# A ninth slot, in two halves, for the ring of expert weights, and a new pairing of the mixing stage's weight buffers

## The reference, cut to what matters

```python
def hierarchical_moe(h, ...):          # T = 256 tokens, 32 experts, top 2 of one group of 8
    ...
    def expert_block(args):
        xb, e = args
        hid = jax.nn.silu(xb @ w_expert_gate[e]) * (xb @ w_expert_up[e])   # 1024 -> 512, twice
        return hid @ w_expert_down[e]                                      # 512 -> 1024
```

```python
    mixed = gates[..., :D] * y_att + gates[..., D:] * y_rwkv
    x = x + mixed @ w_out
```

## Time and profile before

| | us |
|---|---|
| median of 3 runs | 1432.18 |
| lowest and highest | 1431.21 and 1439.7 |
| the profiled execution | 1433.79 |
| its span on the core | 1432.0 |
| PE busy, DVE busy, ACT busy | 1213.7, 734.4, 480.7 |

### The profile page before, as it was taken

How to read it: one execution, slowest core, us unless ns; L and a number is a source line. 1 busy time by engine, 2 the same in 40 slices (tenths; PEclk the granted TensorE clock), 3 DMA queues, 4 the chain that set the end, 5 groups by cost and what they waited for, 6 DMA issues and landing times.

```text
span 1432.0 us, 22429 instructions
## 1 busy us (share of the span) xinstructions
PE 1213.7 (85%) x9471; PEld 959.4 (67%) x9471; DVE 734.4 (51%) x1133; ACT 480.7 (34%) x662; POOL 2.9 (0%) x12
## 2 busy tenths in 40 slices
PE   6999999999474646647466999999999999999998
PEld 6988798796121212213122798799998898899997
DVE  4475754375010101101011698787777798776776
ACT  3443432232000000000000654654445555644544
POOL 0000000000000000000000000000000000000000
PEclk9999999999788867788688999999999999999999
DMA  8841201697999999999999834576665435576650
GB/s 260 281 130 57 75 17 31 215 372 269 423 427 427 427 428 427 427 426 429 426 428 406 262 123 136 146 229 177 187 196 177 133 118 148 158 208 182 195 156 30
DMA packets 180408, 349.68 MB, mean 244 GB/s; under 512 B 8076, under 2 KB 154673, under 8 KB 168786
## 3 DMA queue, kind: packets, MB, share of 16 engines
q1 hardware_dynamic: 179818, 347.59, 67.2%
q10 hardware_dynamic: 488, 0.62, 0.2%
HBM read 347.13 MB, written 3.43 MB: 245 GB/s over the span
## 4 chain that ended last, share of the span: by engine, by line
PE 55%; DMA 18%; DVE 2%; SPq 2%; issue 2%; DVEq 1%; ACT 1%; ACTq 0%
PE ps L2528 25%; DMA expert_ring<-in_w_expert_up 13%; PE ps L2564 11%; PE ps L1769 5%; PE ps L1800 3%; DMA expert_ring<-in_w_expert_down 2%; PE ps L1474 2%; DMA expert_ring<-in_w_expert_gate 2%; PE ps L1814 2%; PE ps L2540 2%; PE ps L1757 2%; SPq L1904 1%; DVE w_lo L2842 1%; PE ps L2488 1%; SPq L1674 1%
## 5 line engine op out<-in xcount | busy, mean ns | idle before, releaser
L1769 PE MATMUL ps<-expert_ring,w_slot 128*32 128x512 f32 x768 | 143.2, 722 | 83.3 <-DMA expert_ring<-in_w_expert_gate 52.4
L2842 DVE TENSOR_TENSOR w_lo<-expert_early,w_hi 128x2048 fp32r<-128x2048 f32 x80 | 182.9, 2291 | 32.2 <-ACT w_hi L2665 30.3
L1842 DVE TENSOR_TENSOR hT<-ps,hT 128x512 f32<-128x512 f32 x8 | 8.5, 1068 | 356.8 <-PE ps L1769 356.8
L2665 ACT ACTIVATE w_hi<-expert_early 128x2048 fp32r<-128x2048 f32 x80 | 153.0, 1918 | 63.1 <-PE ps L2564 35.4
L2528 PE MATMUL ps<-x_hi,w_hi 128*128 128x256 f32 x1024 | 148.5, 284 | 0.0
L2528 PE MATMUL ps<-x_lo,w_hi 128*128 128x256 f32 x1024 | 145.0, 281 | 1.4 <-DVE x_lo L2865 0.7
L2528 PE MATMUL ps<-x_hi,w_lo 128*128 128x256 f32 x1024 | 143.0, 282 | 0.0
L2528 PEld LDWEIGHTS ps<-x_hi,w_hi 128*128 128x128 f32 x1024 | 132.6, 189 | 7.3 <-ACT x_hi L2702 1.8
L1769 PE MATMUL ps<-expert_early,w_slot 128*32 128x512 f32 x256 | 71.7, 723 | 76.3 <-DMA expert_ring<-in_w_expert_up 41.9
L2528 PEld LDWEIGHTS ps<-x_lo,w_hi 128*128 128x128 f32 x1024 | 130.3, 188 | 4.2 <-DVE x_lo L2865 2.9
L2528 PEld LDWEIGHTS ps<-x_hi,w_lo 128*128 128x128 f32 x1024 | 131.0, 190 | 0.0
(11 more groups left out here) (471 smaller groups left out, 1920.8 us busy)
## 6 DMA issues: line engine op xcount, KB each, us to landing
expert_ring<-in_w_expert_gate SPq DMA_DIRECT2D x24, 2048.0 KB, 24.0
expert_ring<-in_w_expert_up SPq DMA_DIRECT2D x24, 2048.0 KB, 24.5
expert_ring<-in_w_expert_down SPq DMA_DIRECT2D x18, 2048.0 KB, 23.8
expert_early<-in_ffn_up SPq DMA_DIRECT2D x36, 1024.0 KB, 6.2
w_slot<-in_w_in SPq DMA_DIRECT2D x28, 1024.0 KB, 5.5
expert_early<-in_w_in SPq DMA_DIRECT2D x20, 1024.0 KB, 5.2
expert_early<-in_ffn_down SPq DMA_DIRECT2D x18, 1024.0 KB, 5.1
expert_early<-in_w_expert_gate SPq DMA_DIRECT2D x8, 2048.0 KB, 15.5
```

The lines of the kernel that those rows point to most:

```text
L1769: mm = pe.matmul(m.ps[rows_of(e), b, :], x_quad[:, k, rows_of(e)], w[e][:, k, :], start=(k == 0), stop=(k == KC - 1))
L2665: act.activation(w_hi[:, half_slot(l, i), :], raw_slot(m, i), ACT.Copy).then_inc(S["w_hi"], 1)
L2842: dve.tensor_tensor(w_lo[:, s, :], raw_slot(m, i), w_hi[:, s, :].bitcast(F32), ALU.subtract).then_inc(S["w_lo"], 1)
```

## The change

- `SLOTS_R` goes from 8 to 9. The ninth slot (`APART`, number 8) is in two halves of 8 KB per partition: one over the last 2048 columns of the constants, one at `room_at`, below the room of the experts' stage, which moves up by 8 KB. A chunk for it is loaded with two issues of 1024 KB, one for each half (`InHalves` gives `expand` and `down` the row that they ask for). Chunks 8, 17, 26, ... 89 fall into it: ten of the 96.
- The order of the early chunks is 3, 4, 8, 5, 6, 7. Mixing's `w_hi` and `w_lo` are paired by piece, so slot 5 holds both parts of one piece and slot 6 those of the other. Chunk 5 waits for `("out", 2, 1)`, chunk 6 for `("out", 3, 1)`.
- Of the first downs, three come in quarters (chunks 9, 10, 11), since chunk 8 is there whole.
- The layers' constants (from `cos` on, 2048 columns, 1024 KB) are loaded behind pieces 0 to 3 of the first layer; TensorE and VectorE wait for them (`const_late`) at the first use. `past` is no longer in the array.
- The overflow's picks lie over the half at `room_at`.

```diff
+LATE_CONST = CONST_AT["cos"][0]
...
-            sp.dma_start(m.const[:, first:], a["const"][:, first:]).then_inc(const_rest, 16)
+            sp.dma_start(m.const[:, first:LATE_CONST], a["const"][:, first:LATE_CONST]).then_inc(const_rest, 16)
...
-    w_hi, w_lo = room("w3_hi", [P, SPLITS, 2 * D], F32R), room("w3_lo", [P, SPLITS, 2 * D], F32R)
+    w_pair = room("w3_pair", [P, SPLITS, 2, 2 * D], F32R)
+    w_hi, w_lo = w_pair[:, :, 0, :], w_pair[:, :, 1, :]
...
+    def pair_of(i):
+        return SPLITS - 1 - i % SPLITS
...
-        for g in range(3, SLOTS_R):
+        for g in (3, 4, APART, 5, 6, 7):
             if g == 3:
                 sp.wait_ge(gated, 4)
             if g == 5:
+                await_filled(sp, ("out", 2, 1))
+            if g == 6:
                 await_filled(sp, ("out", 3, 1))
...
-EARLY, SLOTS_R = 2, 8
+EARLY, SLOTS_R = 2, 9
+APART = SLOTS_R - 1
...
-    sp.dma_start(expert_chunk(m, name, slot)[:, :, :], src).then_inc(m.landed[slot], 16)
+    if slot < APART:
+        sp.dma_start(expert_chunk(m, name, slot)[:, :, :], src).then_inc(m.landed[slot], 16)
+    else:
+        dst = expert_chunk(m, name, slot)
+        for half in range(2):
+            rows = slice(half * dst.rows, (half + 1) * dst.rows)
+            sp.dma_start(dst.halves[half][:, :, :], src[:, rows, :]).then_inc(m.landed[slot], 16)
...
-                    for g in range(SLOTS_R, SLOTS_R + 4):
+                    for g in range(SLOTS_R, SLOTS_R + 3):
...
+                sp.dma_start(m.const[:, LATE_CONST:], a["const"][:, LATE_CONST:]).then_inc(m.const_late, 16)
...
+            if l == 0:
+                dve.wait_ge(m.const_late, 16)
             for h in range(4):
                 b = await_filled(dve, l, "sb_score", h)
...
+            m.apart = [m.const[:, LATE_CONST:], Room(nc, m.room_at)("expert_apart", [P, 2 * D])[:, :]]
```

More of the change, by code:

```diff
@@ L1473, in tiles @@
                     col = k * piece_shape(i)[1] + at
-                    mm = pe.matmul(out, w[:, i % SPLITS, col:col + P], x[y][:, x0 + k, :],
+                    mm = pe.matmul(out, w[:, pair_of(i), col:col + P], x[y][:, x0 + k, :],
                                    start=(p == 0 and k == 0), stop=(p == 2 and k == n - 1))
@@ L1564, in split @@
             await_mix_piece(act, m, i)
-            act.activation(w_hi[:, i % SPLITS, :], raw(i), ACT.Copy).then_inc(split_hi, 1)
+            act.activation(w_hi[:, pair_of(i), :], raw(i), ACT.Copy).then_inc(split_hi, 1)
         def squares(i, c0, c1):
@@ L1593, in split_low @@
             dve.wait_ge(split_hi, i + 1)
-            dve.tensor_tensor(w_lo[:, i % SPLITS, :], raw(i), w_hi[:, i % SPLITS, :].bitcast(F32), ALU.subtract
+            dve.tensor_tensor(w_lo[:, pair_of(i), :], raw(i), w_hi[:, pair_of(i), :].bitcast(F32), ALU.subtract
                               ).then_inc(split_lo, 1)
@@ L1654, with __init__, __getitem__ @@
 QUADS = N_EXP // 4
-EARLY, SLOTS_R = 2, 8
+EARLY, SLOTS_R = 2, 9
+APART = SLOTS_R - 1
+class InHalves:
+    def __init__(self, halves, rows):
+        self.halves = [x.rearrange("p (c n) -> p c n", c=rows // 2) for x in halves]
+        self.rows = rows // 2
+    def __getitem__(self, at):
+        p, row, cols = at
+        return self.halves[row // self.rows][p, row % self.rows, cols]
 def chunk_room(m, slot):
@@ L1663, in expert_chunk @@
 def expert_chunk(m, name, slot):
+    if slot == APART:
+        return InHalves(m.apart, 4 if name == "down" else 8)
     return chunk_room(m, slot).rearrange("p e n -> p (e n)").rearrange("p (c n) -> p c n", c=4 if name == "down" else 8)
@@ L1907, in _ @@
                 for s in range(EARLY):
-                    await_used(sp, QUADS - 1, len(CHUNKS) - SLOTS_R + s)
+                    await_used(sp, QUADS - 1, max(k for k in range(len(CHUNKS)) if ((QUADS - 1) * len(CHUNKS) + k) % SLOTS_R == s))
                     for i in (2 * s, 2 * s + 1):
                         load_piece(sp, m, a, 0, i)
+                assert all(g % SLOTS_R != APART for g in range(last_down, last_down + 4))
+                sp.dma_start(m.const[:, LATE_CONST:], a["const"][:, LATE_CONST:]).then_inc(m.const_late, 16)
                 with sp.If(over > 0):
@@ L1932, in weights @@
                         g = i * len(CHUNKS) + k
-                        if first < 8 or 0 < i < QUADS - 1:
+                        if first < 8 or 0 < i < QUADS - 1 or g == APART:
                             pe.wait_ge(m.landed[g % SLOTS_R], 16 * expert_loads(g))
```

33 lines of the change are left out of this document (19 added, 14 removed).

## The result

| | before | after |
|---|---|---|
| median, us | 1432.18 | 1426.97 |
| lowest and highest, us | 1429.5 to 1439.7 | 1422.57 to 1429.58 |
| profiled execution's span, us | 1432.0 | 1425.1 |

Seven runs each. The ratio of the times is 0.995 with a 95% interval of 0.9935 to 0.9966: 5 to 9 us faster, a small gain that is clear of noise. The medians differ by 5.2 us. The forecast was 1427.9.

The account below looks back on a forecast made before the run. The prediction took the experts' stage to be bound by its loads at 427 GB/s. Terms of -4.9 and +0.6 us summed to -4.3, taking the median from 1432.18 to 1427.9 us, with an 8-in-10 range of 1425 to 1433.

Parts of the forecast that it names:

- The bound: Experts' stage, about 360 to 757 us: bound by its loads' rate, 427 GB/s, not by latency.
- The ninth slot: Start of the experts' stage: one more chunk loaded before gates are used gives the stream 4.9 us of lead.
- Chunk 5 earlier: Issued 8.5 us sooner, it moves the 10.3 us hole in the load stream (321 to 335 us) without closing it: 0.
- the pairing: Mixing's w_hi and w_lo by piece: changes addresses and no wait of ACT, VectorE or TensorE, 0.
- the empty stretch: Sign in the profile after: the DMA queue empty for about 4 us between 342 and 347 us.
- Quarters: First downs, twelve quarter loads instead of sixteen: taken as 0, with bounds of -0.7 and +0.9 us.
- lost lead: Rival at the first quarters: slow restart from an empty queue eats the gain, 1432.4 us; 0.11 together with another rival.
- Halves: Ten chunks in two loads each, 1.3% slower: +0.6 us, with bounds of 0 and 2.1 us.
- each half pays its own start: Rival in slot 8's ten chunks: ten extra loads cost 27 us, giving 1454 us; chance 0.04.
- The constants: Layers' constants: 0 saved at the front; 2.5 us of loading at the end, covered by 13.7 us, so 0.
- The whole hole closed: Rival at the stage's start: chunk 5's early issue counts too, 10.3 us come back, 1422 us; chance 0.03.
- Not loaded ahead: Rival: queue depth holds chunk 8 until after the quarters begin, no gain, 1432 us; 0.11 together with another rival.

Follow-up runs that it names:

- r_before: The kernel before, unchanged, measured against itself; ratio 1.0000, 1434.82 us against 1434.11.
- e1: The kernel before (eight slots) with only w_hi and w_lo paired by piece and chunk 5 issued earlier; ratio 1.0002.
- e3: The kernel before (eight slots) with only the layers' constants loaded late and their unused array left out; ratio 1.0001.
- e7: The kernel before (eight slots) with chunk 7 issued only when the first part of the gates has been used; ratio 1.0019.
- e5: The kernel before (eight slots) with three of the first downs in quarters instead of four, chunk 8 whole behind them; ratio 1.0002.
- e4: The kernel before with each of its 88 whole chunks loaded as two halves of 1024 KB, in the same slots; ratio 1.0038, 1439.36 us.
- r_after: The changed kernel measured again, against the kernel before; ratio 0.9966, 1429.66 us against 1434.18.
- e2: The changed kernel (nine slots) with chunk 8 issued behind chunk 7 instead of behind chunk 4; ratio 0.9974 to the kernel before.
- e8: The changed kernel with the first quarters of chunks 9 and 10 loaded early into room of their own; ratios 0.9963 and, repeated, 0.9957 to the kernel before.

## Why the prediction was right

**The bound.** Right. The rate is 426 to 427 GB/s over the stage in every kernel with whole chunks, and B to C the same within 0.2 us in before, r_before, e1, e3 and e7.

**The ninth slot, -4.9 us.** Right in mechanism, place and price. Between kernels whose queue is empty at the first release, one slot is worth 4.85 us (e7 to e1) and 4.8 to 5.2 us (e1 to the changed kernel). Over all profiles the mean of A to B is 47.97 us with eight slots (five) and 42.04 with nine (three): -5.9, about 1 us more than the term. That microsecond is best put down to the next term. No run has the ninth slot with the old pairing.

**Chunk 5 earlier, 0, and the pairing, 0.** Nearly right. The hole moved to the place that was named; the empty stretch was put at 4 us, and 61 GB/s from 342 to 347 are 4.3 us lost. But the prediction says in one place that the last bytes of the eight slots are arriving at 346.84 us, and in another that chunk 5's early issue fills no slot that was not full by then. The second is not quite so: the kernel before ran at 451 GB/s up to the first release and moved 0.4 MB more from there to B than e1, which is 1 us of stream. In A to B, e1 is 1.1 to 1.9 us shorter than the four others with eight slots. It is one profile of e1, and its ratio (1.0002, with -1.6 to +2.1 us inside the interval) does not show the gain, so the size is an estimate.

**Quarters, 0.** Right within the bounds, by e5. What the prediction says against the lost lead, that the dip at 347 us belongs to the quarters, is not borne out: e7 starts on a whole chunk and has 330 GB/s in the ten microseconds from 1.9 us behind A, where the kernels with eight slots that start on quarters have 295 to 346.

**Halves, +0.6 us.** Right. B to C is 0.5 us longer with nine slots (355.18 against 354.65, the mean without e5), with eight chunks of slot 8 in that distance; e4 gives 0.083 us each, 0.8 us for ten. The rival that each half pays its own start is refuted: 88 more loads cost 5.4 us, not 43 (at 0.49 us each). The Trainium skill, "DMA: Bandwidth & Descriptors", section Anatomy of one DMA — SWDGE (gpsimd) path (not Bandwidth, as the prediction had it), gives about 2.0 us of fixed cost to a transfer that GpSimd issues. By an estimate from that page the 88 would cost 176 us. The 5.4 us measured say that loads of SyncE which stand in a full queue do not pay it one by one.

**The constants, 0 at both ends.** Right as far as e3 can tell (its interval is -2.1 to +2.3 us). From the start of the last scatter's last matmul to the end of the span, the six profiles with early constants took 637.8 to 640.7 us and the six with late ones (e3 and all with nine slots) 639.7 to 640.6. The means are 639.2 and 640.1: a cost of up to 1 us is not excluded, and not shown either.

**The sum.** -4.3 us forecast. The runs gave -7.2 (0.9950 x 1432.18) and -4.9 (0.9966), the stage by A, B and C -5.9 + 0.5 = -5.4. The forecast (a ratio of 0.9970) lies inside one of the two intervals and just above the other. The term that was mis-sized is that of chunk 5, 0 in place of about -1 us. Of the signs that the prediction names, the 390 GB/s and the empty stretch came; the last downs came at 780.05 and not 784.7, since besides the lead A was 1.9 us early and the end of the stage 1.5 us short, both inside the scatter of the executions.

**The rivals.** Lost lead: no, by A to B; and the restart from empty does no harm, since A to B is shorter with an empty queue (after, r_after) than with a running one (e2). The whole hole closed (-10.3): no; e8, which comes nearest to it, is at 0.996. Not loaded ahead: no, chunk 8 is issued at 307 us.

## What to carry to other kernels

In this kernel, the stage that is bound by its loads was shortened only by bytes that were in before its first release. Count the slots that are full at that moment, and price them at the rate of the full stream. Filling a hole in the queue without more room behind it moves the hole, and gains no more than the part of a chunk that was still landing. To see such a gain, measure from the first use of a load (A) to the first wait that a load ends (B), and the stream's rate from there to a later wait of the same kind (C). Two executions of one kernel differed by 0.3 to 0.5 us in A to B and by at most 0.3 us in B to C, and by up to 5.5 us in their whole spans.

## What the runs showed of the hardware

- A full queue's rate goes down by a few per cent with smaller loads: 427 GB/s with 2048 KB and rows of 16 KB per partition, 420 with 1024 KB and 8 KB (e4), 409 to 413 where loads of 512 KB with 4 KB are under way, at a DMA share of 1.01 to 1.03 in each. Size and row change together here. An extra load in such a queue costs 0.06 us by the whole time of e4 and 0.083 us by B to C.
- In the ten microseconds behind the first release the queue moves 243 to 346 GB/s, in all twelve executions: with the queue empty ahead of it (e1, after) or still running (before, e2), on quarters or on a whole chunk (e7). Except in e8, issues come fast enough for more. No run says why.
- TensorE's mean granted clock between 75 and 125 us was 0.93, 0.97 and 1.00 in executions of kernels that are the same there (before, r_before, e7), and 0.96 or 1.00 at the start of the layers.
- The same output product of mixing, 140 matmuls in one piece of the chain, took between 17.05 and 19.78 us from execution to execution, with either pairing of its buffers.
